# Key and value slots: a weight's low part made half by GpSimd and half by VectorE, the query's normed tiles spread over sixteen slots

## What is computed

```python
def _mem_kv(mem, g_mem, w_k_mem, w_v_mem):
    mn = _rms(mem, g_mem)
    mk = (mn @ w_k_mem).reshape(B, N_MEM, N_XHEADS, XHEAD_DIM)
    mv = (mn @ w_v_mem).reshape(B, N_MEM, N_XHEADS, XHEAD_DIM)
...
    h = x + mix
    h = h + _cross_attn(_rms(h, p["g_norm_x"]), mem_k, mem_v, p["w_q_x"], p["w_o_x"])
```

## Time and profile before

| | us |
|---|---|
| median of 3 runs | 1926.26 |
| lowest, highest | 1923.93, 1930.83 |
| profiled execution | 1925.1 |
| its span, first to last instruction | 1923.3 |
| TensorE busy in the span | 1693.7 (88%) |
| VectorE busy | 811.0 (42%) |
| GpSimd busy | 645.1 (34%) |
| ScalarE busy | 458.1 (24%) |
| mean granted TensorE clock | 0.924 of full speed |

### The profile page before, as it was taken

The page is one execution under the profiler, slowest core; times in us unless marked ns, Lnnn a source line. Parts: engine busy times, 40 slices in busy tenths (PEclk is TensorE's granted clock), DMA queues, the critical chain, the costliest instruction groups (busy, mean ns, idle before and its releaser), DMA issues.

```text
span 1923.3 us, 41083 instructions
## 1 busy us (share of the span) xinstructions
PE 1693.7 (88%) x17220; PEld 1548.2 (80%) x17220; DVE 811.0 (42%) x1101; ACT 458.1 (24%) x665; POOL 645.1 (34%) x380
## 2 busy tenths in 40 slices
PE   4899996898877999998889887987969999999996
PEld 3889985898526999996359777973859999999995
DVE  3059999103496555555332562022551111111127
ACT  3222221123451111110112223242123311221221
POOL 2345555435462000000025347310334443443442
PEclk8899998899767999999669898999979999999997
DMA  2212225223300000203103223345112222222222
GB/s 110 71 60 76 65 66 56 65 93 113 116 1 2 4 4 4 45 12 103 76 11 120 78 75 111 132 156 230 55 33 77 76 76 77 66 83 70 75 78 86
DMA packets 54715, 139.93 MB, mean 73 GB/s; under 512 B 22193, under 2 KB 24753, under 8 KB 52561
## 3 DMA queue, kind: packets, MB, share of 16 engines
q1 hardware_dynamic: 53328, 133.08, 22.6%
q0 software_dynamic: 1280, 5.24, 0.7%
HBM read 125.32 MB, written 12.99 MB: 72 GB/s over the span
## 4 chain that ended last, share of the span: by engine, by line
PE 66%; DVE 13%; issue 10%; POOL 4%; ACT 3%; DMA 1%; DVEq 1%; SPq 0%; POOLq 0%; ACTq 0%; PEldq 0%
PE ps L335 43%; PE ps L443 14%; DVE acc L1219 4%; PE ps L1655 3%; POOL wlo L315 3%; PE ps L1596 1%; PE ps L376 1%; DVE x L756 1%; DVE tmp L1231 1%; PE ps L1704 1%; PE ps L1731 1%; DVE p_L L1295 1%; DMA kc<-in_kc 1%; PE ps L1643 1%; DMA wmask<-in_wmask 1%
## 5 line engine op out<-in xcount | busy, mean ns | idle before, releaser
L315 POOL TENSOR_TENSOR wlo<-raw,whi 128x1024 fp32r<-128x1024 f32 x174 | 443.7, 2550 | 476.5 <-ACT whi L304 476.2
L335 PE MATMUL ps<-xnl,whi 128*128 128x320 f32 x800 | 189.9, 319 | 54.5 <-POOL wlo L315 32.1
L304 ACT ACTIVATE whi<-raw 128x1024 fp32r<-128x1024 f32 x174 | 183.7, 1056 | 225.0 <-PE ps L335 212.5
L335 PEld LDWEIGHTS ps<-xnl,whi 128*128 128x128 f32 x800 | 136.1, 193 | 63.1 <-POOL wlo L315 31.0
L335 PE MATMUL ps<-xnh,wlo 128*128 128x320 f32 x800 | 185.9, 314 | 0.0
L335 PE MATMUL ps<-xnh,whi 128*128 128x320 f32 x800 | 185.8, 314 | 0.0
L335 PE MATMUL ps<-fnl,whi 128*128 128x320 f32 x704 | 162.9, 313 | 14.4 <-POOL fnl L400 14.1
L335 PE MATMUL ps<-fnh,whi 128*128 128x320 f32 x704 | 162.4, 312 | 0.0
L335 PE MATMUL ps<-fnh,wlo 128*128 128x320 f32 x704 | 162.2, 312 | 0.0
L1219 DVE SCALAR_TENSOR_TENSOR acc<-up,vec,acc 128x512 f32<-128x512 f32 x240 | 160.3, 739 | 0.0
L1525 POOL TENSOR_TENSOR yol<-po,yoh 128x640 fp32r<-128x640 f32 x8 | 12.3, 1534 | 394.1 <-ACT yoh L1063 394.1
(11 more groups left out here) (298 smaller groups left out, 3343.7 us busy)
## 6 DMA issues: line engine op xcount, KB each, us to landing
raw<-in_slots SPq DMA_DIRECT2D x174, 512.0 KB, 3.6
kc<-in_kc SPq DMA_DIRECT2D x4, 2048.0 KB, 8.5
vc<-in_vc SPq DMA_DIRECT2D x8, 1024.0 KB, 7.2
xin<-in_x SPq DMA_DIRECT2D x4, 640.0 KB, 6.0
tmp_g<-tmp POOLq DMA_DIRECT2D x8, 320.0 KB, 2.5
tmp_m<-pr POOLq DMA_DIRECT2D x8, 320.0 KB, 4.3
m1t<-tmp_m SPq DMA_DIRECT2D x1, 2560.0 KB, 11.7
t2t<-tmp_g SPq DMA_DIRECT2D x1, 2560.0 KB, 17.7
```

The costliest lines, as they stand in the source:

```text
L304: nc.scalar.activation(whi[s][:].rearrange("p a b -> p (a b)"), raw[s][:], ACT.Copy).then_inc(S["w_hi"], 1)
L315: nc.gpsimd.tensor_tensor(wlo[s][:].rearrange("p a b -> p (a b)"), raw[s][:], whi[s][:].rearrange("p a b -> p (a b)").bitcast(F32), ALU.su ...
L335: last = nc.tensor.matmul(cut(ps[s], h, n), a[:, k, :], b[:, k, h * w:(h + 1) * w], start=(k == 0 and q == 0), stop=(k == k_tiles - 1 and ...
```

## The change

In the last seven key slots, the eight value slots and the first query slot (16 slots), the low part of a slot is made in two halves of 512 columns: GpSimd the first, VectorE the second, each after ScalarE's high part (`lo_half`). VectorE counts its halves in a new semaphore `w_lo_dve`, which it also raises by one right after the reciprocal of the query's norm. TensorE waits for both counts in every key and value slot and before the query slots, the first key slot included, where the count it wants is that one. SP loads a slot when both halves of the slot two before are made; these loads are written out one by one (`load_shared`).

The query's eight normed tiles are no longer made in the key slots, one a slot, but over the key and value slots, one for each pair: ScalarE makes the high tile after the eviction of the pair's second slot, GpSimd the low tile after its two halves, VectorE the normed tile between its two halves, in a single buffer.

```diff
@@ -264,7 +264,7 @@
             return a.rearrange("p (b c) -> p b c", b=NS)
 
 
-        names = """consts_in w_hi w_lo mm_done params sq_ready sq_part sq_summed ms_ready std_ready rstd_ready xn_ready
+        names = """consts_in w_hi w_lo w_lo_dve mm_done params sq_ready sq_part sq_summed ms_ready std_ready rstd_ready xn_ready
...
@@ -286,6 +286,16 @@
         block = ctx.enter_context(nc.Block())
 
 
+        SHARED = SLOTS["mk"][0] + 1
+
+        def load_shared(sp, lo, hi):
+
+            for m in range(lo, hi):
+                sp.wait_ge(S["w_lo"], m - 1)
+                if m - 2 < SHARED + 2 * DT:
+                    sp.wait_ge(S["w_lo_dve"], m - SHARED)
+                sp.dma_start(raw[m % 2][:], io["slots"][m]).then_inc(raw_in[m % 2], 16)
+
         def load_slots(sp, lo, hi):
 
             with sp.Fori(0, (hi - lo) // 2) as i:
@@ -314,6 +324,14 @@
             pool.wait_ge(S["w_hi"], 2 * i + (m + 1))
             nc.gpsimd.tensor_tensor(wlo[s][:].rearrange("p a b -> p (a b)"), raw[s][:],
                                     whi[s][:].rearrange("p a b -> p (a b)").bitcast(F32), ALU.subtract).then_inc(S["w_lo"], 1)
+
+        def lo_half(eng, pool, i, m):
+
+            s, h = m % 2, slice(0, 512) if pool else slice(512, 1024)
+            eng.wait_ge(S["w_hi"], 2 * i + (m + 1))
+            sub = nc.gpsimd.tensor_tensor if pool else nc.vector.tensor_tensor
+            sub(wlo[s][:].rearrange("p a b -> p (a b)")[:, h], raw[s][:, h], whi[s][:].rearrange("p a b -> p (a b)")[:, h].bitcast(F32),
+                ALU.subtract).then_inc(S["w_lo"] if pool else S["w_lo_dve"], 1)
 
         def dense(pe, stage, hi, lo, k_tiles=DT, n=NT, part=None, split=None):
 
@@ -326,6 +344,8 @@
             with pe.Fori(0, cnt // 2) as i:
                 for s in range(2):
                     pe.wait_ge(S["w_lo"], 2 * i + (n0 + s + 1))
+                    if stage in ("mk", "mv"):
+                        pe.wait_ge(S["w_lo_dve"], 2 * i + (n0 + s + 2 - SHARED))
                     pe.wait_ge(psum_free[s], i + (n0 // 2 + 1))
                     for k in range(k_tiles):
                         if split and s == 0:
@@ -901,12 +921,14 @@
             load_slots(sp, SLOTS["out"][0], SLOTS["out"][0] + 2)
             sp.wait_ge(S["mg_ready"], DT)
             sp.dma_start(memt[:], io["mem"]).then_inc(S["mem_in"], 16)
-            load_slots(sp, SLOTS["out"][0] + 2, SLOTS["q"][0] + 2)
+            load_slots(sp, SLOTS["out"][0] + 2, SLOTS["mk"][0] + 2)
+            load_shared(sp, SLOTS["mk"][0] + 2, SLOTS["q"][0] + 2)
             sp.wait_ge(S["mk_in"], DT)
             sp.dma_start(io["mk"], mkt[:]).then_inc(S["all_stored"], 16)
             sp.wait_ge(S["mvt_in"], DT)
             sp.dma_start(io["mv"], mvt[:]).then_inc(S["all_stored"], 16)
-            load_slots(sp, SLOTS["q"][0] + 2, SLOTS["ox"][0] + 2)
+            load_shared(sp, SLOTS["q"][0] + 2, SLOTS["q"][0] + 4)
+            load_slots(sp, SLOTS["q"][0] + 4, SLOTS["ox"][0] + 2)
             sp.wait_ge(S["q_in"], DT)
             sp.dma_start(xmask[:], io["xmask"]).then_inc(S["xm_in"], 16)
             for p in range(4):
@@ -1088,8 +1110,7 @@
                         nc.scalar.activation(tile_of(dst, 2 * i + s), ps[s][:, 0:NMEM], ACT.Copy).then_inc(done, 1)
                         act.wait_ge(done, 2 * i + (s + 1))
                         act.sem_inc(psum_free[s], 1)
-                        if stage == "mk":
-                            high_tile(act, 2, 2 * i + s, s, hnh, n2_bufs)
+                    high_tile(act, 2, i + (4 if stage == "mv" else 0), 0, hnh, n2_bufs)
             n0 = SLOTS["q"][0]
             with act.Fori(0, 4) as i:
                 for s in range(2):
@@ -1394,7 +1415,16 @@
             added, squared = [0], [0]
             dve.wait_ge(S["res_in"], 16)
             add_residual("out", n2_bufs)
-            norm_dve(dve, 2, lambda k: ht[:, k, :], "g_norm_x", n2_bufs)
+            stats_dve(dve, 2, n2_bufs)
+            dve.sem_inc(S["w_lo_dve"], 1)
+            for half, stage in enumerate(("mk", "mv")):
+                n0 = SLOTS[stage][0]
+                with dve.Fori(0, 4) as i:
+                    lo_half(dve, False, i, n0 + 1)
+                    dve.wait_ge(S["xl_ready"], i + (2 * DT + 4 * half))
+                    nc.vector.scalar_tensor_tensor(out=n2_bufs[3][0][:], in0=tile_of(ht, i + 4 * half), scalar=v1("g_norm_x", i + 4 * half),
+                                                   in1=n2_bufs[2][:], op0=ALU.mult, op1=ALU.mult).then_inc(S["xn_ready"], 1)
+                    lo_half(dve, False, i, n0 + 2)
 
             for i in range(4):
                 s = i % 2
@@ -1534,11 +1564,14 @@
                 n0 = SLOTS[stage][0]
                 with pool.Fori(0, 4) as i:
                     for s in range(2):
-                        lo_part(pool, i, n0 + s + 1)
+                        if stage in ("mk", "mv"):
+                            lo_half(pool, True, i, n0 + s + 1)
+                        else:
+                            lo_part(pool, i, n0 + s + 1)
                         if stage == "out":
                             low_tile(pool, 1, 2 * i + s, s, memh, meml, n2_bufs, NMEM)
-                        if stage == "mk":
-                            low_tile(pool, 2, 2 * i + s, s, hnh, hnl, n2_bufs)
+                    if stage in ("mk", "mv"):
+                        low_tile(pool, 2, i + (4 if stage == "mv" else 0), 0, hnh, hnl, n2_bufs)
             n0 = SLOTS["ox"][0]
             with pool.Fori(0, 4) as i:
                 for s in range(2):
@@ -1662,6 +1695,7 @@
             pe.wait_ge(S["xl_ready"], 2 * DT)
             dense(pe, "mk", memh, meml, n=NMEM)
             dense(pe, "mv", memh, meml, n=NMEM)
+            pe.wait_ge(S["w_lo_dve"], 2 * DT + 1)
             dense(pe, "q", hnh, hnl, split=("xl_ready", 2 * DT))
 
             for s in range(2):
```

## The result

| kernel | median, us | runs | ratio to before, 95% interval |
|---|---|---|---|
| before | 1926.20 | 20 | 1 |
| changed | 1930.59 | 20 | 1.0022 (1.0013 to 1.0031) |

The changed kernel is 0.22% slower, 4.2 us by the ratio. That is inside the 0.3% called "no change", inside the range of 1921 to 1934, and 2.6 us above the 1928.0 that was forecast. One of its 20 runs took 1990.23 us, at a granted clock of 0.82, and is left out of the ratio. The profiled execution is 1928.9 us long from its first to its last instruction, 5.6 more than before.

A forecast was written before the change was run, and what follows sets the result against it. TensorE's idle time and lower clock in the key and value slots were taken as the bound. A 3.2 us gain at full clock and 5.2 of clock falls made +2.0; with 1.2 to the median, forecast 1928.0, range 1921 to 1934.

The forecast's parts named there:

- The start: First key slot: TensorE waits for VectorE's count after the reciprocal, so its matmuls begin near 1139.3, 5.9 us late.
- The halves in turn: Low parts of the slots: GpSimd and VectorE take turns, so both halves cost 1.70 us where the whole cost 2.36.
- The period: Key and value stages: 8.28 us between second slots, seven periods; query stage starts 3.2 us earlier at full clock.
- The falls of the clock: Second slots behind 2.3 us of TensorE idling: clock falls in 3.5 of 7 periods at 1.5 us, 5.2 in all.
- The four gaps of 2.36 in the first stage: TensorE gaps of 2.35 to 2.37 us, two followed by a lower clock, two not; taken as guide for half falling.
- Sum: Whole kernel: -3.2 + 5.2 = +2.0 us, taking the profiled 1925.1 to 1927.1.
- the first rival's case: Second slot of each pair: clock falls after nearly every gap, 1.5 us each, +5.8 with six falls; chance 0.16.
- the forecast's two to five falls: Over the seven periods: two to five falls of the clock, -0.2 to +4.3 us; chance 0.60.
- The overlap rival: Both halves run at once, 1.28 us in place of 1.70; period 7.86, no falls, -6.1 us, 1920.2; chance 0.10.
- The clock stays up: Key and value periods: none or one fall of the clock, -3.2 to -1.7 us, 1923.1 to 1924.6; chance 0.14.
- Hidden terms: Loads, stores and last normed tile cost nothing; that tile is finished 3.3 us after the last value slot, needed after 6.2.

The follow-up runs named there:

- e1: The changed kernel with VectorE's count of one given before the reciprocal of the norm instead of after it; 1928.46 us, ratio 1.0008 to before.
- e10: The changed kernel with VectorE's half subtracting 512 columns of PSUM in place of the weight's high part in SBUF; 1925.66 us, ratio 0.9995 to before.
- e2: The changed kernel with ten unused filler matmuls on TensorE after the first slot of every pair; 1925.67 us, ratio 1.0003 to before.
- e3: The changed kernel without halves: GpSimd makes each low part whole, no new wait at the start, tiles still spread over sixteen slots; 1932.75 us, ratio 1.0030 to before.
- e5: The changed kernel with VectorE making the whole low part of the sixteen slots, GpSimd keeping only the tiles; 1918.00 us, ratio 0.9956 to before.
- e4: The changed kernel with the halves kept but the normed tiles put back in the key slots, one a slot; 1928.64 us, ratio 1.0003 to before.

## Why the prediction was right

- **The start.** Forecast: first matmul near 1139.3 and second key slot 5.5 late. Measured against the norm's root, the second slot's eviction is 5.3 late. Right; e1 recovered 3.7 of it by moving one count.
- **The halves in turn.** Forecast 1.70 and 0.14 to the matmul; measured 1.95 together. Right in kind, 0.1 short. e10 shows the cause: with one SBUF operand less on VectorE both halves run at once (1144.99 and 1145.04). The Trainium skill, page "SBUF — State Buffer", section "SBUF: two separate sides", names the two SBUF inputs as the condition; e10 agrees, 0.69 beside 1.28 where the changed kernel has 0.69 and 1.78.
- **The period.** Forecast 8.28 at full clock, measured 8.38. Seven times the difference is 0.7, so the gain at full clock was not 3.2 but 2.5. e2 agrees: its stage is 1.6 shorter than before, after 1.05 was spent on the filler's delay in the first pair.
- **The falls of the clock.** This is the term that was mis-sized. Forecast: half of the seven periods, 1.5 each, 5.2 in all. Price right (1.1 to 1.5). Number: in the profiled execution a fall followed each of the six idle stretches of 2.36 to 2.42, 8.4 in all; only the first period, whose idle time came in two pieces of 1.0 and 1.1, had none. The four gaps of 2.36 in the first stage, with another pattern of work around them, were a poor guide.
- **Sum.** Forecast +2.0; in the profiled pair +5.6 between the spans, and +6.0 in the stage (-2.4 as measured at full clock, +8.4 of falls). That is the first rival's case (-3.2 + 9.0 = +5.8), which had a chance of 0.16, and not the forecast's two to five falls. The median rose by 4.4 (4.2 by the ratio). It rose by less than the profiled execution because that of the kernel before, 1925.10, lay 1.1 below its median, while that of the changed kernel, 1930.61, lies on its own. The forecast had added 1.2 for the first and expected the same of the second. So the median is 2.6 above the forecast where the profiled execution is 3.5 above its 1927.1: that part of the closeness is luck. The range held because it took in the case of all falls.
- **The overlap rival** is refuted by the changed kernel's own rows and by e10. "The clock stays up" is what e2 made, and there, with the filler, no gain over the kernel before can be told either, 1.0003.
- **Hidden terms.** The loads, the stores and the last normed tile stayed hidden: the last second slot's eviction (1213.00) is 7.4 us ahead of the query's first, in which 7.07 is that slot's own work.

## What to carry to other kernels

An instruction that is halved between two engines is shorter only as far as the engines can run together: look in the trace for the same two side by side before counting on it, and try giving the whole to the faster one. Before making a link of a chain shorter, ask whether it has to stand on the chain: moving one line of ScalarE's order was worth 15 us, the falls of the clock included, the halves with their late start some 2 in the order as it stood (the changed kernel against e3). A count that gates a buffer should not stand behind unrelated work on the engine that gives it, and an idle stretch of TensorE can cost the clock behind it as well as itself (here 1.1 to 1.5 us on top of 2.4).

## What the runs showed of the hardware that was not expected

- Which idle stretches cost the clock cannot be read from their length alone. The six of 2.36 to 2.42 in the changed kernel were each followed by a fall, those of 1.60 to 1.63 in e5 and of 1.20 to 1.23 in e2 by none. Between them stands e10, whose timeline of TensorE gives the stretches before three of its second slots:

```profile
1158.78 0.36 PE L356 MATMUL ps<-meml,whi 128*128 128x256 f32 x1 [1.94 <-POOL wlo L333]
...
1177.44 0.36 PE L356 MATMUL ps<-meml,whi 128*128 128x256 f32 x1 [1.77 <-POOL wlo L333]
...
1194.78 0.36 PE L356 MATMUL ps<-meml,whi 128*128 128x256 f32 x1 [1.91 <-POOL wlo L333]
```

  The slot at 1158.78, and three more behind 1.93 to 1.97, took 4.6 to 4.7 to their eviction, those at 1177.44 and 1194.78 only 3.24. But e1 has a stretch of 2.24 (and two of 2.23) with no fall behind it, and e4, in its key slots, one of 1.94 with a fall:

```profile
1158.71 0.36 PE L355 MATMUL ps<-meml,whi 128*128 128x256 f32 x1 [2.24 <-POOL wlo L333]
```

```profile
1158.32 0.38 PE L355 MATMUL ps<-meml,whi 128*128 128x256 f32 x1 [1.94 <-POOL wlo L333]
```

  The first of these slots, of e1, took 3.23 to its eviction, the second, of e4, 4.75. What decides besides the length was not tried.
- GpSimd's whole part, VectorE's whole part and the two in turn cost 2.36, 1.23 and 1.95 (to the matmul) for the same subtraction.
- The rest of the program behind the query's first eviction took from 707.8 to 712.8 us in the twelve profiles, with no relation to the edits that can be seen; most of the spread arises between the query and the feed-forward part. There it goes with the granted clock, as the windows over the same 709 matmuls show, first in the kernel before, then in e1 (columns as in the earlier trace rows):

```profile
1272.62:1422.45 149.83, 120.12 (x709) 89.06 (x708) 66.60 (x74) 35.44 (x74) 19.32 (x8) 0.93 0.35 130
```

```profile
1273.82:1428.40 154.58, 124.74 (x709) 91.70 (x707) 66.59 (x74) 35.38 (x74) 19.28 (x8) 0.90 0.34 126
```

  The spread is as large as the effect studied, so a single span says little without the stage beside it. What makes the clock differ there was not tried.
